# Split branch outputs taken straight from the banks of their transposes, with unit splits and a memset in other places of three stages

## The chip, the cores and the metric

The kernel runs on 1 core of one Trainium2 chip. The metric is the device time in microseconds (us) of one execution. Engines are called TensorE (PE in the profile, PEld its weight load), VectorE (DVE), ScalarE (ACT), GpSimd (POOL) and SyncE (SP).

## What is computed

Two layers of a decoder trunk over 256 tokens of width 1024, in float32. The reference, cut to the part that the change touches:

```python
for layer in range(DEPTH):                      # 2
    h = rms_norm(x, norm_mix[layer])
    proj = h @ w_in[layer]                      # qkv and gates of three branches
    o_a = gated_deltanet(...)                   # branch A, (1, 256, 512)
    o_b = hgrn2(...)                            # branch B
    o_c = dilated_attention(...)                # branch C, three groups of four heads
    mix = (gates[:, :, 0] * (o_a @ w_br_a[layer])
           + gates[:, :, 1] * (o_b @ w_br_b[layer])
           + gates[:, :, 2] * (o_c @ w_br_c[layer]))
    x = x + mix @ w_out[layer]
    h = rms_norm(x, norm_ffn[layer])
    # layer 0: x += SwiGLU(h); layer 1: x += top 2 of 8 SwiGLU experts
```

o_a and o_b end in `rms_norm(o, norm_g)` times a gate; norm_g is a gain per channel.

## The kernel before, in words

Each large product is made of three float32r products: both operands are split into a high and a low part, and hi x hi, hi x lo and lo x hi are added up (`products`, lines 466 to 470). The weights stream in **units** of 1 MB. SyncE loads unit u into one of 6 raw slots; ScalarE copies it to one of 3 `hi` slots (`prep`, line 1062), for which unit u-3 must have been used by TensorE; VectorE subtracts and leaves the low part in the raw slot (`prep`, line 1506); TensorE waits for both (`unit_ready`) and gives the unit back (`unit_over`). Each engine has its own instruction stream, written out by hand; `prep(n)` says at which places of it the next n units are split. The order of work is this order in the three streams and the semaphores between them; there is no planner.

One mixer layer uses 56 units. They are counted here from 0 in each layer.

**Branch A** (`deltanet`): TensorE transposes its output, normed and gated, into banks 4 and 5 (`turn_output`, line 694). ScalarE copies the two banks, times the gain, to the float32 tile `oT` (line 1266).

**Branch B** (`hgrn`): VectorE makes 1-f (`b_k`, line 1807), a clamp (line 1809), a memset of the attention tile (line 1811), one unit split, a running sum (line 1816) and a first difference. Then come turns n = 0 to 7: VectorE makes the two operands `b_qe` and `b_ke` of score product n+1, the next difference, a masked copy of score product n, and a unit split (two in turn 0). TensorE does score product n and one unit of 24 products in each turn (two units in turn 0), units 18 to 27 in all. After the last turn come the value products (24 matmuls), and ScalarE takes `b_o` out of banks 4 and 5, for norm and gate (`output_norm`).

**Branch C, first part** (`dilated`, the loop over three groups): TensorE uses six units in a turn (q, k, v of a group; units 28 to 45). ScalarE waits for branch B's output ahead of the loop (line 1307). In one turn ScalarE and VectorE split two units, square and norm q, split two, norm k, split two.

**Between the loop and the scores**: the halves of the split output of branch A, `o_hi[0]` and `o_lo[0]`, lie in the memory of `actT_hi`, and those of branch B in that of `actT_lo`; these are the operands of all of the input's products. So `split_branch(L, 0)` (ScalarE line 1338 and 1392, VectorE line 1878 and 1964) waits until unit 45 has been used, and splits `oT` there. Branch B's output is transposed after the loop too, copied to `oT`, and split after it (lines 1373 and 1930).

**Branch C, second part**: a loop written out, eight turns n (line 799), one for each of four heads in two blocks of tokens. TensorE: scores n+1, transposes of p, half a unit of branch A's or B's projection (`branch_part`, units 46 to 49), values n. VectorE: scaled scores n+1, and in even turns the gated product, then a unit split, and at the end of the turn `c_o` (line 1947), the output of head n. The transposes of the first block of `c_o` (`turn_oc`, line 811) come in turn 5. Units 50 to 55 follow in `project`.

In the last stage experts' chosen tokens are split into `e_hi` and `e_lo`, and their results into `y_hi` and `y_lo`.

Of the kernel before, what the change touches and what calls it, by code (L numbers as in the profile page):

```python
# [22 lines left out]
P = 128  # L23
# [128 lines left out]
def build(ctx, nc, dram):  # L152
# [44 lines left out]
    oT = sb("oT", [P, 3, H, T])  # L197
# [19 lines left out]
    b_o = sb("b_o", [P, TT, W], at=t0 + 8192)  # L217
# [15 lines left out]
    o_hi = [sb(f"o_hi{n}", [P, H, T], F32R, at=o0 + 8192 * n) for n in range(2)]  # L233
    o_lo = [sb(f"o_lo{n}", [P, H, T], F32R, at=o0 + 8192 * n + 4096) for n in range(2)]
    oc_hi = sb("oc_hi", [P, H, T], F32R, at=t0)
    oc_lo = sb("oc_lo", [P, H, T], F32R, at=t0 + 4096)
# [132 lines left out]
    oT_made = signal("oT_made", 2)  # L369
# [90 lines left out]
    def _(pe):  # L460
# [233 lines left out]
        def turn_output(L, br, src):  # L694

            pe.wait_ge(o_made.sem, o_made.at(L, br))
            for h in range(H):
                for t in range(TT):
                    a = src[:, t, h, :] if len(src.shape) == 4 else src[:, t, hs(h)]
                    ins = pe.transpose(PS[:, (4, 2)[br] + h // 2, ((h % 2) * TT + t) * P:((h % 2) * TT + t + 1) * P],  # L700
                                       a, ident)
# [3 lines left out]
        def hgrn(L):  # L705
# [3 lines left out]
            for n in range(LEVELS + 2):  # L709
# [27 lines left out]
        def dilated(L):  # L737
# [80 lines left out]
        def branch_c(L, k, t, js):  # L818
# [237 lines left out]
    def _(act):  # L1056
# [209 lines left out]
        def turn_output(L, br):  # L1266
            act.wait_ge(o_T.sem, o_T.at(L, 2 * br + 1))
            col = (R_GA, R_GB)[br] + L
            act.activation(oT[:, br, :, :].rearrange("p a b -> p (a b)"), bank(*((4, 5), (2, 3))[br]), COPY,
                           scale=small[:, col:col + 1]).then_inc(oT_made.sem, 1)  # L1270

        def hgrn(L):
# [22 lines left out]
            for n in range(LEVELS + 2):  # L1295
                prep(1 if n else 2)
# [9 lines left out]
        def dilated(L):  # L1306
            act.wait_ge(o_made.sem, o_made.at(L, 1))
            with prog.loop(act, GROUPS, 2) as g:
# [16 lines left out]
                prep(2)  # L1325
# [46 lines left out]
            act.wait_ge(oT_made.sem, oT_made.at(L, 1))  # L1372
            split_branch(L, 1)
            for n in range(TT * H):
# [3 lines left out]
                if n % 2 == 0:  # L1378
# [969 lines left out]
```

## Time and profile before

| | before |
|---|---|
| median of 3 runs (lowest to highest) | 2156.52 us (2156.25 to 2160.19) |
| the profiled execution, its own time | 2160.02 us |
| its span, first to last instruction | 2158.2 us |
| mean granted TensorE clock | 0.981 of full speed |
| TensorE, VectorE, ScalarE busy | 96%, 75%, 57% of the span |

The profiled execution is one of its own, beside the three runs. In rows of instructions the first number is the start in us from the start of the span, the second the duration; a pair of brackets at the end gives the time that the engine stood idle before the row and what ended it. Layer 0 of the mixers lies at about 20 to 460 us, layer 1 at 660 to 1108 us, experts behind it.

### The profile page before, as it was taken

Reading aid. Unit: us, or ns where it says so; the run is one execution under the profiler, and the core shown is the slowest. Engines: PE = TensorE matmul, PEld = TensorE weight load, DVE = VectorE, ACT = ScalarE, POOL = GpSimd, SP = SyncE. Lnnn points to the kernel's source line nnn. Section 1 sums busy time; section 2 is a strip of 40 time slices with the busy share of each in tenths; the row PEclk is TensorE's granted clock in tenths of the full one; section 3 lists DMA queues with packets and bytes.
Section 4 is the critical chain, followed back from the end, with each engine's and each line's share of the span. In section 5 each row is a group of like instructions: output and inputs, shape, how many; then the busy total and the mean of one; then the engine's idle time right before and its main releaser. Section 6 shows DMA issues by size and latency. Waiting matters only on the chain.

```text
span 2158.2 us, 29174 instructions
## 1 busy us (share of the span) xinstructions
PE 2065.2 (96%) x10899; PEld 1752.1 (81%) x10899; DVE 1612.2 (75%) x1256; ACT 1240.0 (57%) x1017; POOL 6.7 (0%) x12
## 2 busy tenths in 40 slices
PE   7999999989998999999979999999999999999997
PEld 6997887779997997887767888888888888888885
DVE  5878855745445878855766888898888889888886
ACT  4544455344433544455346767777676777767674
POOL 0000000000000000000000000000000000000000
PEclk9999999989999999999989999999999999999998
DMA  8423454245564523455237999999999999999995
GB/s 274 157 79 98 137 189 161 85 142 194 177 193 128 175 79 98 137 188 163 80 126 273 369 330 366 344 351 370 325 369 326 369 345 350 366 329 369 330 367 187
DMA packets 239201, 512.25 MB, mean 237 GB/s; under 512 B 11391, under 2 KB 34039, under 8 KB 239132
## 3 DMA queue, kind: packets, MB, share of 16 engines
q1 hardware_dynamic: 238124, 507.60, 67.6%
q0 software_dynamic: 1008, 3.69, 0.5%
q8 instruction: 48, 0.79, 0.2%
q14 instruction: 21, 0.17, 0.0%
HBM read 510.19 MB, written 1.07 MB: 237 GB/s over the span
## 4 chain that ended last, share of the span: by engine, by line
PE 85%; DVE 8%; issue 3%; ACT 2%; DMA 0%; DVEq 0%; SPq 0%; ACTq 0%
PE PS L468 25%; PE PS L470 25%; PE PS L469 25%; PE PS L539 6%; DVE lo L1511 3%; PE PS L940 1%; PE PS L977 1%; ACT hi L1070 1%; PE PS L488 1%; PE PS L953 0%; DVE a_act L1612 0%; DVE x L2031 0%; PE PS L750 0%; DMA rows<-in_knorm_c 0%; DVE t_n L1534 0%
## 5 line engine op out<-in xcount | busy, mean ns | idle before, releaser
L1511 DVE TENSOR_TENSOR lo<-raw,hi 128x2048 fp32r<-128x2048 f32 x481 | 1096.0, 2290 | 332.6 <-ACT hi L1070 329.5
L1070 ACT ACTIVATE hi<-raw 128x2048 fp32r<-128x2048 f32 x481 | 920.7, 1916 | 419.4 <-PE PS L470 413.7
L468 PE MATMUL PS<-hi,e_hi 128*128 128x512 f32 x896 | 358.7, 400 | 1.4 <-DVE e_lo L1534 1.4
L469 PE MATMUL PS<-lo,e_hi 128*128 128x512 f32 x896 | 354.3, 395 | 0.0
L470 PE MATMUL PS<-hi,e_lo 128*128 128x512 f32 x896 | 354.2, 395 | 0.0
L468 PE MATMUL PS<-hi,actT_hi 128*128 128x512 f32 x640 | 253.9, 397 | 2.9 <-ACT gate L1280 1.4
L470 PE MATMUL PS<-hi,actT_lo 128*128 128x512 f32 x640 | 249.6, 390 | 0.0
L469 PE MATMUL PS<-lo,actT_hi 128*128 128x512 f32 x640 | 249.1, 389 | 0.0
L468 PE MATMUL PS<-hi,fT_hi 128*128 128x512 f32 x536 | 210.1, 392 | 3.0 <-DVE fT_lo L1534 1.8
L469 PE MATMUL PS<-lo,fT_hi 128*128 128x512 f32 x536 | 209.2, 390 | 0.0
L470 PE MATMUL PS<-hi,fT_lo 128*128 128x512 f32 x536 | 208.9, 390 | 0.0
L468 PEld LDWEIGHTS PS<-hi,e_hi 128*128 128x128 f32 x896 | 169.1, 189 | 40.2 <-DVE e_lo L1534 1.6
L470 PEld LDWEIGHTS PS<-hi,e_lo 128*128 128x128 f32 x896 | 169.0, 189 | 40.2
L469 PEld LDWEIGHTS PS<-lo,e_hi 128*128 128x128 f32 x896 | 169.3, 189 | 37.7
L468 PE MATMUL PS<-actT_hi,hi 128*128 128x256 f32 x672 | 192.1, 286 | 2.5 <-DVE actT_lo L1585 1.4
L469 PE MATMUL PS<-actT_lo,hi 128*128 128x256 f32 x672 | 190.9, 284 | 0.0
L470 PE MATMUL PS<-actT_hi,lo 128*128 128x256 f32 x672 | 190.9, 284 | 0.0
L468 PEld LDWEIGHTS PS<-hi,actT_hi 128*128 128x128 f32 x640 | 120.4, 188 | 27.6 <-issue 4.3
L470 PEld LDWEIGHTS PS<-hi,actT_lo 128*128 128x128 f32 x640 | 120.1, 188 | 25.6
L469 PEld LDWEIGHTS PS<-lo,actT_hi 128*128 128x128 f32 x640 | 120.5, 188 | 23.9 <-issue 0.2
L468 PEld LDWEIGHTS PS<-actT_hi,hi 128*128 128x128 f32 x672 | 129.8, 193 | 4.0 <-DVE actT_lo L1585 1.8
L469 PEld LDWEIGHTS PS<-actT_lo,hi 128*128 128x128 f32 x672 | 129.8, 193 | 0.6 <-issue 0.2
(313 smaller groups left out, 2241.5 us busy)
## 6 DMA issues: line engine op xcount, KB each, us to landing
raw<-in_moe_w SPq DMA_DIRECT2D x336, 1024.0 KB, 5.1
raw<-in_w_in SPq DMA_DIRECT2D x92, 1024.0 KB, 5.1
raw<-in_ffn_w SPq DMA_DIRECT2D x33, 1024.0 KB, 5.3
raw<-in_w_br SPq DMA_DIRECT2D x12, 1024.0 KB, 5.1
raw<-in_w_out SPq DMA_DIRECT2D x8, 1024.0 KB, 5.2
hankel<-hankel_dram POOLq DMA_DIRECT2D x1, 1536.0 KB, 13.5
x<-in_x SPq DMA_DIRECT2D x2, 512.0 KB, 4.0
gain<-in_norm_mix POOLq DMA_DIRECT2D x2, 512.0 KB, 5.9
```

The costliest lines, as they stand in the source:

```text
L468: pe.matmul(out, a_hi, b_hi, start=first, stop=False, skip_group_check=True)
L469: pe.matmul(out, a_hi, b_lo, start=False, stop=False, skip_group_check=True)
L470: return pe.matmul(out, a_lo, b_hi, start=False, stop=last, skip_group_check=True)
L488: ins = pe.transpose(PS[:, 4 + j, (2 * kk + t) * P:(2 * kk + t + 1) * P], tile(t, k), ident)
L539: return pe.matmul(out, a, b, start=first, stop=last)
L940: ins = pe.matmul(PS[:, 6 + k // 4, (k % 4) * P:(k % 4 + 1) * P], src[:, t, k * P:(k + 1) * P], pick_r[:, t, :], start=t == 0 and part == ...
L977: ins = pe.transpose(PS[:, 2, j * P:(j + 1) * P], f_g[0][:, j * P:(j + 1) * P], ident)
L1070: act.activation(hi[prog.u % SPLIT][:, :], raw[slot][:, :], COPY).then_inc(hi_made.sem, 1)
L1511: dve.tensor_tensor(lo[prog.u % RAW][:, :], raw[prog.u % RAW][:, :], hi[s][:, :].bitcast(F32), ALU.subtract).then_inc(lo_made.sem, 1)
```

## The change

Branch A's output is transposed into banks 6 and 7 rather than 4 and 5. ScalarE copies these banks, times the gain, to `o_hi[0]` (float32r), and VectorE makes `o_lo[0]` from the same banks in `split_output(L, 0)`, both at the start of `hgrn`. The tiles take the place of `oT`. TensorE waits for the low part ahead of score product 1 (which writes banks 6 and 7), where before it waited for `oT` ahead of score product 0. Branch B's output is split in the same way from banks 2 and 3 after the loop, into the memory of `actT_hi`. Branch C's output later uses the tiles of branch A.

The memset of `b_attn` moves from the start of `hgrn` into turn 0, and one of the two unit splits of turn 0 goes; the loop over the groups splits three units ahead of the first norm and one after the second; in the eight turns a unit is split in turns 0, 1, 2, 4 and 6, and on VectorE it stands after `c_o`. The experts' split tiles move to the memory of `actT_hi` and `actT_lo`.

```diff
-    oT = sb("oT", [P, 3, H, T])
+    oa_hi = sb("oa_hi", [P, H, T], F32R)
+    oa_lo = sb("oa_lo", [P, H, T], F32R)
+    b_o = sb("b_o", [P, TT, W])
...
-    o_hi = [sb(f"o_hi{n}", [P, H, T], F32R, at=o0 + 8192 * n) for n in range(2)]
-    o_lo = [sb(f"o_lo{n}", [P, H, T], F32R, at=o0 + 8192 * n + 4096) for n in range(2)]
-    oc_hi = sb("oc_hi", [P, H, T], F32R, at=t0)
-    oc_lo = sb("oc_lo", [P, H, T], F32R, at=t0 + 4096)
+    o_hi = [oa_hi, sb("ob_hi", [P, H, T], F32R, at=o0)]
+    o_lo = [oa_lo, sb("ob_lo", [P, H, T], F32R, at=o0 + 4096)]
...
-    e_hi = sb("e_hi", [P, KT, P], F32R)
+    e_hi = sb("e_hi", [P, KT, P], F32R, at=o0)
...
 TensorE, turn_output
-                    ins = pe.transpose(PS[:, (4, 2)[br] + h // 2, ...
+                    ins = pe.transpose(PS[:, (6, 2)[br] + h // 2, ...
 TensorE, hgrn
-                    if n == 0:
-                        pe.wait_ge(oT_made.sem, oT_made.at(L, 0))
+                    if n == 1:
+                        pe.wait_ge(o_lo_made.sem, o_lo_made.at(L, 0))
 TensorE, values
                 if n == 0:
-                    pe.wait_ge(oT_made.sem, oT_made.at(L, 1))
+                    pe.wait_ge(o_lo_made.sem, o_lo_made.at(L, 1))
 ScalarE, turn_output
-            act.activation(oT[:, br, :, :].rearrange("p a b -> p (a b)"), bank(*((4, 5), (2, 3))[br]), COPY,
-                           scale=small[:, col:col + 1]).then_inc(oT_made.sem, 1)
+            act.activation(flat(o_hi[br]), bank(*((6, 7), (2, 3))[br]), COPY,
+                           scale=small[:, col:col + 1]).then_inc(o_hi_made.sem, 1)
 ScalarE, hgrn
             for n in range(LEVELS + 2):
-                prep(1 if n else 2)
+                prep(1)
 ScalarE, dilated, the loop over groups
-                prep(2)
+                prep(3)
                 square(0)
...
                 turned_c(1)
-                prep(1)
-
-            used(L, U_C + 18)
-            split_branch(L, 0)
             turn_output(L, 1)
...
             exps(0)
-            act.wait_ge(oT_made.sem, oT_made.at(L, 1))
-            split_branch(L, 1)
             for n in range(TT * H):
...
-                if n % 2 == 0:
+                if n % 2 == 0 or n == 1:
                     prep(1)
 VectorE, hgrn
-            dve.memset(flat(b_attn), 0.0).then_inc(dve_step.sem, 1)
-            dve.wait_ge(dve_step.sem, prog.step())
+            split_output(L, 0)
             prep(1)
...
+                if n == 0:
+                    dve.memset(flat(b_attn), 0.0).then_inc(dve_step.sem, 1)
+                    dve.wait_ge(dve_step.sem, prog.step())
                 masked(n)
-                prep(1 if n else 2)
+                prep(1)
 VectorE, dilated
-                prep(2)
+                prep(3)
                 normed(0)
                 prep(2)
                 normed(1)
-                prep(2)
-
-            split_branch(L, 0)
+                prep(1)
...
             scaled(0)
-            split_branch(L, 1)
+            split_output(L, 1)
             for n in range(TT * H):
...
                 if n % 2 == 0:
                     gated(L, n // 2, 3)
-                    prep(1)
...
                 dve.wait_ge(c_oc.sem, c_oc.at(L, n))
+                if n % 2 == 0 or n == 1:
+                    prep(1)
...
+        def split_output(L, br):
+
+            col = (R_GA, R_GB)[br] + L
+            dve.wait_ge(o_hi_made.sem, o_hi_made.at(L, br))
+            dve.scalar_tensor_tensor(flat(o_lo[br]), bank(*((6, 7), (2, 3))[br]), small[:, col:col + 1],
+                                     flat(o_hi[br]).bitcast(F32), ALU.mult, ALU.subtract).then_inc(o_lo_made.sem, 1)
```

## Rows read from the trace of the kernel before

**Rows 1.** The page's first part: busy us, share and instructions of each engine.

```profile
PE 2065.2 (96%) x10899; PEld 1752.1 (81%) x10899; DVE 1612.2 (75%) x1256; ACT 1240.0 (57%) x1017; POOL 6.7 (0%) x12
```

**Rows 2.** The waits of TensorE: total us, times, longest us.

```profile
PE PS L468 <- DVE o_lo L1534: 8.6, 2, 4.3
...
PE PS L815 <- DVE c_o L1947: 3.9, 2, 1.9
```

**Rows 3.** Timeline of TensorE, score products 2 and 8 of branch B, both layers.

```profile
207.83 3.58 PE L539 MATMUL PS<-b_qe,b_ke 128*128 128x128 f32 x16 [2.04 <-DVE b_ke L1534]
...
253.36 1.16 PE L539 MATMUL PS<-b_qe,b_ke 128*128 128x128 f32 x8
...
856.73 2.05 PE L539 MATMUL PS<-b_qe,b_ke 128*128 128x128 f32 x16 [2.04 <-DVE b_ke L1534]
...
901.03 1.16 PE L539 MATMUL PS<-b_qe,b_ke 128*128 128x128 f32 x8
```

**Rows 4.** Windows: length, busy us of each engine, granted clock, DMA share, GB/s.

```profile
208.00:212.00 4.00, 4.00 (x19) 3.92 (x20) 3.93 (x3) 1.26 (x2) 0.00 (x0) 0.57 0.61 233
373.50:378.00 4.50, 4.42 (x10) 3.47 (x11) 2.58 (x6) 1.66 (x3) 0.00 (x0) 0.50 0.00 0
1021.20:1026.00 4.80, 4.75 (x11) 3.78 (x12) 2.56 (x5) 1.66 (x3) 0.00 (x0) 0.50 0.00 0
```

**Rows 5.** Timeline of VectorE, start of branch B and turn 0, layer 0.

```profile
183.95 0.69 DVE L1809 TENSOR_SCALAR b_f<-b_f 128x1024 f32<-128x1024 f32 x1
185.03 1.34 DVE L1811 MEMSET b_attn<- 128x1536 f32 x1 [0.39 <-DVE b_f L1809]
...
188.62 2.86 DVE L1816 TENSOR_TENSOR_SCAN b_gc<-tiny,b_f 128x256 f32<-128x256 f32 x4
...
200.89 4.49 DVE L1511 TENSOR_TENSOR lo<-raw,hi 128x2048 fp32r<-128x2048 f32 x2
```

**Rows 6.** Timeline of ScalarE, start of branch B, layer 0.

```profile
183.15 1.12 ACT L1269 ACTIVATE oT<-PS,small 128x1024 f32<-128x1024 f32 x1 [3.70 <-PE PS L700]
184.16 1.91 ACT L1070 ACTIVATE hi<-raw 128x2048 fp32r<-128x2048 f32 x1
...
187.38 1.06 ACT L1276 ACTIVATE b_f<-b_f 128x1024 f32<-128x1024 f32 x1
```

**Rows 7.** Timelines of TensorE, ScalarE and VectorE, end of branch B, start of the group loop, layer 0.

```profile
259.85 2.84 PE L539 MATMUL PS<-b_i,b_attn 128*128 128x128 f32 x24
263.38 0.47 PE L468 MATMUL PS<-hi,actT_hi 128*128 128x512 f32 x1 [0.69 <-ACT gate L1280]
...
274.36 0.39 PE L468 MATMUL PS<-hi,actT_hi 128*128 128x512 f32 x1
...
260.10 1.91 ACT L1070 ACTIVATE hi<-raw 128x2048 fp32r<-128x2048 f32 x1 [4.57 <-PE PS L470]
...
262.82 1.02 ACT L1303 ACTIVATE b_o<-PS 128x1024 f32<-128x1024 f32 x1
...
270.84 1.92 ACT L1070 ACTIVATE hi<-raw 128x2048 fp32r<-128x2048 f32 x1 [2.79 <-DVE b_o L1534]
...
272.79 2.29 DVE L1511 TENSOR_TENSOR lo<-raw,hi 128x2048 fp32r<-128x2048 f32 x1 [2.23 <-ACT hi L1070]
```

**Rows 8.** Timelines of VectorE and TensorE, after the group loop, layer 0.

```profile
372.31 1.22 DVE L1534 TENSOR_TENSOR o_lo<-oT,o_hi 128x1024 fp32r<-128x1024 f32 x1
...
373.58 0.80 PE L468 MATMUL PS<-hi,o_hi 128*128 128x512 f32 x1 [4.33 <-DVE o_lo L1534]
```

**Rows 9.** Timelines of VectorE and ScalarE, turns 0 and 1 of the eight, layer 0.

```profile
373.44 0.42 DVE L1890 SCALAR_TENSOR_TENSOR c_s<-PS,bias 128x256 f32<-128x256 f32 x1
373.89 0.29 DVE L1895 SCALAR_TENSOR_TENSOR c_s<-PS,bias 128x128 f32<-128x128 f32 x1
...
374.99 0.61 ACT L1354 ACTIVATE c_p<-c_s,stat 128x384 f32<-128x384 f32 x1 [2.98 <-DVE stat L1900]
...
382.84 1.22 DVE L1972 SCALAR_TENSOR_TENSOR gate<-gate,PS 128x1024 f32<-128x1024 f32 x1 [1.56 <-PE PS L470]
```

More of the change, by code:

```diff
@@ L216, in build @@
     b_e = sb("b_e", [P, H, T], at=c0 + 6144)
-    b_o = sb("b_o", [P, TT, W], at=t0 + 8192)
     b_o2 = sb("b_o2", [P, TT, W], at=c0 + 14336)
@@ L261, in build @@
     pickT = sb("pickT", [P, TT, P], F32R)
-    e_hi = sb("e_hi", [P, KT, P], F32R)
-    e_lo = sb("e_lo", [P, KT, P], F32R)
-    y_hi = sb("y_hi", [P, D], F32R)
-    y_lo = sb("y_lo", [P, D], F32R)
+    e_hi = sb("e_hi", [P, KT, P], F32R, at=o0)
+    e_lo = sb("e_lo", [P, KT, P], F32R, at=o0 + 4096)
+    y_hi = sb("y_hi", [P, D], F32R, at=o0 + 8192)
+    y_lo = sb("y_lo", [P, D], F32R, at=o0 + 12288)
     PS = ctx.enter_context(nc.psum_tensor("PS", [P, 8, 512], F32))
@@ L368, in build @@
     o_T = signal("o_T", 6)
-    oT_made = signal("oT_made", 2)
     bf_read = signal("bf_read")
@@ L699, in turn_output @@
                     a = src[:, t, h, :] if len(src.shape) == 4 else src[:, t, hs(h)]
-                    ins = pe.transpose(PS[:, (4, 2)[br] + h // 2, ((h % 2) * TT + t) * P:((h % 2) * TT + t + 1) * P],
+                    ins = pe.transpose(PS[:, (6, 2)[br] + h // 2, ((h % 2) * TT + t) * P:((h % 2) * TT + t + 1) * P],
                                        a, ident)
@@ L825, in branch_c @@
             for j in js:
-                ins = products(PS[:, (6, 0)[k] + t, :], oc_hi[:, j, t * P:(t + 1) * P],
-                               oc_lo[:, j, t * P:(t + 1) * P], unit_view(w_hi, 4)[:, j, :],
+                ins = products(PS[:, (6, 0)[k] + t, :], o_hi[0][:, j, t * P:(t + 1) * P],
+                               o_lo[0][:, j, t * P:(t + 1) * P], unit_view(w_hi, 4)[:, j, :],
                                unit_view(w_lo, 4)[:, j, :], first=j == 0, last=j == H - 1)
@@ L1360, in split_oc @@
                 act.wait_ge(o_T.sem, o_T.at(L, 4 + t))
-                act.activation(oc_hi[:, :, t * P:(t + 1) * P], PS[:, 2, :].rearrange("p (h j) -> p h j", h=H),
+                act.activation(o_hi[0][:, :, t * P:(t + 1) * P], PS[:, 2, :].rearrange("p (h j) -> p h j", h=H),
                                COPY).then_inc(o_hi_made.sem, 1)
@@ L1388, in dilated @@
             prep(1)
-        def split_branch(L, br):
-            act.activation(flat(o_hi[br % 2]), oT[:, br, :, :].rearrange("p a b -> p (a b)"),
-                           COPY).then_inc(o_hi_made.sem, 1)
         def dense():
@@ L1905, in split_oc @@
                 v = slice(t * P, (t + 1) * P)
-                tt(oc_lo[:, :, v], bank4(2), oc_hi[:, :, v].bitcast(F32), ALU.subtract).then_inc(o_lo_made.sem, 1)
+                tt(o_lo[0][:, :, v], bank4(2), o_hi[0][:, :, v].bitcast(F32), ALU.subtract).then_inc(o_lo_made.sem, 1)
             def gated_c(k, t):
@@ L1960, in dilated @@
             prep(2)
-        def split_branch(L, br):
+        def split_output(L, br):
+            col = (R_GA, R_GB)[br] + L
             dve.wait_ge(o_hi_made.sem, o_hi_made.at(L, br))
-            tt(flat(o_lo[br % 2]), oT[:, br, :, :].rearrange("p a b -> p (a b)"),
-               flat(o_hi[br % 2]).bitcast(F32), ALU.subtract).then_inc(o_lo_made.sem, 1)
+            dve.scalar_tensor_tensor(flat(o_lo[br]), bank(*((6, 7), (2, 3))[br]), small[:, col:col + 1],
+                                     flat(o_hi[br]).bitcast(F32), ALU.mult, ALU.subtract).then_inc(o_lo_made.sem, 1)
         def gated(L, k, pair):
```

## The prediction

> **What bounds the kernel.** I read the page's first part: TensorE is busy for 96% of the span, VectorE for 75% [rows 1]. So the time is TensorE's work plus its stops and slow stretches, and only what shortens those counts. The list of TensorE's waits and its timeline give three that this change touches: 8.6 us in two stops for `o_lo`, 3.9 us in two stops for `c_o` [rows 2], and two stops of 2.04 for `b_ke` [rows 3]; one of each in each layer. They lie ahead of score product 2 of branch B [rows 3], ahead of the first product of branch A's projection [rows 8], and at the transposes of `c_o` in turn 5. Windows of the clock show what a stop costs beyond itself [rows 4]: behind the 4.3 us stops TensorE ran at 1.2 GHz (0.50) for at least 4.5 and 4.8 us; behind the 2.0 us stop it was at 0.57 over 4 us in layer 0, while in layer 1 the same product took 2.05 us rather than 3.58 [rows 3], so was at full clock. Stops of 2 us can thus cost clock, or not.
>
> **Change, part 1: start of branch B.** VectorE's chain from 183.95 to 207.8 has no idle time to speak of. The memset took 1.34 us after 0.39 of start [rows 5]. The new split in its place starts at 184.66, since `o_hi` is ready at 184.3 [rows 6], and I take 1.22 us, the price of another three-operand instruction on two banks [rows 9]. A split between SBUF tiles took 1.22 too [rows 8]. Bounds: 0.69 (a one-operand instruction of that size, rows 5) to 2.3 (twice the elements, rows 5). It ends at 185.9; the unit split then waits for ScalarE's `hi` until 186.1 and ends at 188.4; the running sum waits for ScalarE's logarithm, which ends at 188.44 [rows 6]. So it starts at 188.5 rather than 188.62: 0.15 us are gained, not 0.4, since ScalarE is late next. Turn 0 then loses one of two unit splits (4.49 for two, so 2.2, rows 5) and gains the memset (1.35). Together `b_ke` of turn 1 comes 0.15 + 2.2 - 1.35 = 1.0 us sooner. TensorE's stop shrinks from 2.04 to 1.0.
>
> What of it lasts? In layer 1 product 2 to product 8 took 44.3 us, 7.38 per turn [rows 3]. A unit of 24 products takes 5.49 (half of 274.36 - 263.38, rows 7) and 16 score matmuls 1.8, together 7.3: VectorE sets the pace by a hair, and whatever it gains early arrives at the end. Layer 1 gains 1.0. In layer 0 the same stretch took 45.5 because of the slow clock. A stop of 1.0 should not slow it: 1.0 + 1.2 = 2.2. TensorE's new wait for `o_lo` ahead of product 1 costs nothing: it is made 12 us sooner; behind it only product 1 is queued. Banks 6 and 7 are free, as product 1 is their next writer.
>
> **Part 2: end of branch B.** One unit fewer is now ahead. ScalarE's split at 260.10, which waited 4.57 us for TensorE and kept the last gate and so TensorE's first product of the loop waiting (0.69) [rows 7], is one unit earlier in number and waits for nothing: that 0.69 goes. But unit 30, split there before, is now the first split behind ScalarE's wait for branch B's output. Its `hi` starts where unit 31's did, at 270.84, its low part ends where 272.79 + 2.29 = 275.08 stands, both 0.1 sooner since `b_o` no longer waits for the gate [rows 7]. TensorE comes from its value products (262.69) through two units (10.98) to 273.67, and **stops for 1.3 us**, a new stop. It goes on at 275.0 rather than 274.36: +0.65 in each layer. In the loop the order of splits against norms is as before (three, two, one instead of two, two, two, over the turn's border), and I put it at nothing: TensorE's six units cover it, and the units stay two ahead. If that cover is gone it costs a stop like the 1.3 in each of three turns.
>
> **Part 3: after the loop.** The splits of `oT` (VectorE's is 1.22, rows 8), the wait for unit 45 and the unit split ahead of them leave the path: `o_lo[0]` is made a hundred us earlier. TensorE goes from score product 0 straight into the projection: -4.33 and -4.3. The slow clock behind it goes as well: half of 4.5 and of 4.8 us [rows 4], -2.25 and -2.4. Branch B's split (copy 1.1, low part 1.22) lies under the first half unit; values 0 waits for it, 6 us later.
>
> **Part 4: the eight turns.** With `c_o` ahead of the unit split, the transposes in turn 5 should not stop for 1.94. But a fifth split stands in turn 1. Worked there: from the maximum of scores 2 come ScalarE's exponential (0.61 and some 0.1 for its sum), its `hi` (1.92, rows 7), VectorE's low part (2.29), scaled scores 3 (0.42 + 0.29) [rows 9] and hand-overs of 0.1 to 0.2 in all, 5.8 us, where TensorE has 4.6 of work (half a unit 2.75, the rest small products): a stop of 1.2. Going through all turns like this I find stops of 0.5, 1.2, 0.4, 1.3 and 0.9, 4.3 us, in turns 1 to 4, none in turn 5. The same walk in the old order gives 4.3 as well (the trace has 3.8). I take **0**, with 2 us a layer either way as bounds.
>
> Moved tiles of the experts carry no instruction and no wait: 0. No DMA is added or moved; SyncE's loads follow the use of raw slots, six ahead, and POOL waits for the same fourth low part.
>
> **A rule against the change.** The rows show 1.22 us for 1024 elements from SBUF and from banks alike [rows 8, 9]. The Trainium skill, "VectorE: DVE Perf Modes", section on the TRN2 errata, gives an instruction a larger fixed cost if it reads PSUM (120 cycles against 58). By it each of four splits would cost some 0.06 us more, an estimate from that page, and the sum would be 0.1 to 0.25 us less of a gain. The trace does not agree for this size.
>
> **Sum.** Layer 0: -2.2 + 0.65 - 4.33 - 2.25 = -8.1. Layer 1: -1.0 + 0.65 - 4.3 - 2.4 = -7.1. Together -15.2, from the profiled execution's 2160.0 (span 2158.2 and 1.8 around it): 2144.8. That execution is 3.5 above the median of 2156.5; the slow clock of layer 0 at 208 us, 1.2 of my sum, need not be in the others, as layer 1 shows. From the median I take off 14.0: **2142.5 us**.
>
> **Rivals.**
> 1. *The new stops cost clock.* The 1.3 us stop at unit 30, or those of turns 2 to 4 close together, bring 1.2 GHz in both layers, at about 2.3 us each [rows 4]: 2147. For it: 2.04 did so once. Against: once only, and that was longer. Chance 0.15.
> 2. *The next wait takes the place.* TensorE still stops for 4.3 us after the loop, for scores or for VectorE. Then 4.3 + 2.3 stay in both layers: 2142.5 + 13.3 = 2155.8, no change to be seen. Against: the copy for scores 0 is ready, and scaled scores 0 come sooner, as nothing is queued ahead of them. Chance 0.04.
> 3. *More.* Unit 30 is not late, or the eight turns gain their 1.94: 2142.5 - 2.6 or - 3.9, so 2139. Chance 0.14.
> 4. *Slower: the missing unit.* In branch B's turns a unit is split one turn before its use; `hi` and low part take 4.2 of 7.4 us, so 3.2 are in hand. If raw data or ScalarE come later than that, each of 8 turns and 3 loop turns waits in both layers. It outweighs the gain from 14 / 22 = 0.65 us per turn; at 1.3 us, as at unit 30, it gives 2142.5 + 28 = 2171. Against: ScalarE stood idle for 4.57 us with all tiles full [rows 7]. Chance 0.02.
>
> **How the numbers follow.** Forecast 0.65. About 0.2% (4.3 us) can be told from no change: 2152.2 is the border. Faster: forecast, rivals 1 and 3, together 0.94, less 0.01 for several small ones at once: 0.93. Same: rival 2 and that 0.01: 0.05. Slower: 0.02. The range: forecast with 2 us either way per layer in the turns, half of rival 1's cost beyond it and rival 3's gain: 2138 to 2148.5.
>
> **What would show it.** Right: no wait of TensorE for `o_lo` of some 4 us; the projection's first products at clock 1.00; the stop at product 2 about 1.0 and at full clock; a new stop for `lo` of 1.3 us some 11 us into the group loop; no wait for `c_o` in turn 5 but several of about 1 us for `c_s` and `c_p`. Wrong: a stop of 3 us or more after the loop, waits for `lo` in more than one turn of the loop, or the memset's place on VectorE making product 2 later than before.

## The result, and the profile after

| | before | after |
|---|---|---|
| median of 4 runs (lowest to highest) | 2156.44 us (2156.25 to 2160.19) | 2128.22 us (2127.38 to 2129.13) |
| ratio of the runs, with its 95% interval | | 0.9859 (0.9848 to 0.9871) |
| the profiled execution, its own time | 2160.02 us | 2127.89 us |
| its span | 2158.2 us | 2126.1 us |
| mean granted TensorE clock | 0.981 | 0.988 |

The time fell by 28.2 us, twice the forecast 14.0. In lines of the kernel after, `prep` is L1068 on ScalarE and L1499 on VectorE, the products are L466 to L468, the small matmuls L537. First the page's busy times, which answer to [rows 1]: TensorE lost 24 us of busy time with the same number of matmuls.

```profile
PE 2041.0 (96%) x10899; PEld 1742.6 (82%) x10899; DVE 1610.7 (76%) x1256; ACT 1234.3 (58%) x1013; POOL 6.7 (0%) x12
```

TensorE's waits after, total, times and longest. No `o_lo` and no `c_o` is left of [rows 2]; the waits for `lo` hold the new stops at unit 30.

```profile
PE PS L466 <- DVE lo L1499: 7.5, 11, 1.5
...
PE PS L537 <- DVE c_s L1884: 3.7, 4, 1.0
...
PE PS L537 <- DVE b_ke L1522: 2.9, 2, 1.4
...
PE PS L779 <- ACT c_p L1349: 2.4, 4, 0.7
```

The timeline of TensorE after, at score product 2 of both layers (against [rows 3]) and at unit 30, the third of the group loop (against [rows 7]).

```profile
207.05 2.05 PE L537 MATMUL PS<-b_qe,b_ke 128*128 128x128 f32 x16 [1.43 <-DVE b_ke L1522]
...
273.06 0.47 PE L466 MATMUL PS<-hi,actT_hi 128*128 128x512 f32 x1 [1.54 <-DVE lo L1499]
...
845.76 2.05 PE L537 MATMUL PS<-b_qe,b_ke 128*128 128x128 f32 x16 [1.43 <-DVE b_ke L1522]
...
911.80 0.47 PE L466 MATMUL PS<-hi,actT_hi 128*128 128x512 f32 x1 [1.54 <-DVE lo L1499]
```

Both stops are those forecast (1.0 and 1.3 us), a little longer. Windows of the kernel after, in the same three places as [rows 4] (length, busy times, granted clock, DMA share, GB/s): the clock stays at 1.00 where it was 0.57, 0.50 and 0.50.

```profile
207.00:211.00 4.00, 3.95 (x25) 3.59 (x26) 3.90 (x3) 2.68 (x3) 0.00 (x0) 1.00 0.80 256
369.00:373.50 4.50, 4.50 (x26) 3.85 (x25) 3.29 (x8) 1.59 (x4) 0.00 (x0) 1.00 0.08 30
1009.00:1014.00 5.00, 5.00 (x32) 4.41 (x31) 2.61 (x7) 2.77 (x6) 0.00 (x0) 1.00 0.00 0
```

**Where the time went.** The row that ends branch A (transposes of `t_n`) and the first transposes of each norm (`fn`, `hn`) cut the span into stages. TensorE's timeline before, then after:

```profile
182.02 0.66 PE L700 MATMUL PS<-consts,t_n 128*128 128x128 f32 x4 [0.81 <-DVE t_n L1534]
...
465.14 3.67 PE L488 MATMUL PS<-consts,fn 128*128 128x128 f32 x16 [6.76 <-DVE fn L1552]
668.35 1.97 PE L488 MATMUL PS<-consts,hn 128*128 128x128 f32 x8 [9.30 <-DVE hn L1552]
1113.31 3.03 PE L488 MATMUL PS<-consts,fn 128*128 128x128 f32 x13 [6.76 <-DVE fn L1552]
```

```profile
181.85 0.88 PE L698 MATMUL PS<-consts,t_n 128*128 128x128 f32 x6 [0.82 <-DVE t_n L1522]
...
456.58 3.68 PE L486 MATMUL PS<-consts,fn 128*128 128x128 f32 x16 [6.75 <-DVE fn L1540]
657.98 3.67 PE L486 MATMUL PS<-consts,hn 128*128 128x128 f32 x16 [9.30 <-DVE hn L1540]
1095.33 3.47 PE L486 MATMUL PS<-consts,fn 128*128 128x128 f32 x16 [6.75 <-DVE fn L1540]
```

| stage (from row to row, the last to the span's end) | before | after | difference |
|---|---|---|---|
| mixer 0 behind branch A | 283.12 | 274.73 | -8.4 |
| dense stage | 203.21 | 201.40 | -1.8 |
| mixer 1 | 444.96 | 437.35 | -7.6 |
| last norm and experts | 1044.9 | 1030.8 | -14.1 |

The stages and 0.2 us ahead of them make up the 32.1 us between the two profiled spans; the medians differ by 28.2, as the profiled execution before was 3.6 above its median. The mixers gained 16.0 us, where the sum had 15.2. The other 16 us lie in stages in which, by the forecast, nothing moves; most of it with the experts. TensorE's groups of products there, before and then after (count, busy us, mean ns, idle time before them):

```profile
L468 PE MATMUL PS<-hi,e_hi 128*128 128x512 f32 x896 | 358.7, 400 | 1.4 <-DVE e_lo L1534 1.4
L469 PE MATMUL PS<-lo,e_hi 128*128 128x512 f32 x896 | 354.3, 395 | 0.0
L470 PE MATMUL PS<-hi,e_lo 128*128 128x512 f32 x896 | 354.2, 395 | 0.0
```

```profile
L466 PE MATMUL PS<-hi,e_hi 128*128 128x512 f32 x896 | 354.8, 396 | 1.4 <-DVE e_lo L1522 1.4
L468 PE MATMUL PS<-hi,e_lo 128*128 128x512 f32 x896 | 349.8, 390 | 0.0
L467 PE MATMUL PS<-lo,e_hi 128*128 128x512 f32 x896 | 349.4, 390 | 0.0
```

And a window of 950 us in that stage, before, then after: the clock is 1.00 and TensorE busy for over 99.7% in both, but it did 4390 matmuls instead of 4333.

```profile
1150.00:2100.00 950.00, 948.32 (x4333) 776.01 (x4332) 823.67 (x482) 680.69 (x455) 0.00 (x0) 1.00 0.97 352
```

```profile
1150.00:2100.00 950.00, 947.61 (x4390) 785.45 (x4389) 832.33 (x485) 689.59 (x460) 0.00 (x0) 1.00 0.97 355
```

The 2688 products take 13.2 us less in sum (1067.2 against 1054.0), 4.9 ns each. In such a product (128x512) TensorE holds 128 columns of the split tokens and streams 512 of the split weight, so the suspect is the one part of the change that carries no instruction: the place of `e_hi` and `e_lo`.

### The profile page after: what moved, and what is told of

It reads as the page before. It is cut to its first block, busy times and chain, and to the rows that moved or that the text cites. A ratio compares the mean times of both kernels' runs of the same rounds, so it can differ in the third digit from the quotient of the medians.

```text
span 2126.1 us, 29178 instructions
## 1 busy us (share of the span) xinstructions
PE 2041.0 (96%) x10899; PEld 1742.6 (82%) x10899; DVE 1610.7 (76%) x1256; ACT 1234.3 (58%) x1013; POOL 6.7 (0%) x12
## 4 chain that ended last, share of the span: by engine, by line
PE 85%; DVE 8%; issue 3%; ACT 2%; DMA 0%; DVEq 0%; SPq 0%; ACTq 0%
PE PS L466 25%; PE PS L468 24%; PE PS L467 24%; PE PS L537 7%; DVE lo L1499 3%; PE PS L938 1%; PE PS L975 1%; ACT hi L1068 1%; PE PS L486 1%; PE PS L748 0%; DVE x L2022 0%; DVE a_act L1600 0%; PE PS L951 0%; DMA rows<-in_knorm_c 0%; PE PS L779 0%
## 5 line engine op out<-in xcount | busy, mean ns | idle before, releaser
L1499 DVE TENSOR_TENSOR lo<-raw,hi 128x2048 fp32r<-128x2048 f32 x481 | 1094.6, 2289 | 301.1 <-ACT hi L1068 298.5
L1068 ACT ACTIVATE hi<-raw 128x2048 fp32r<-128x2048 f32 x481 | 919.4, 1915 | 339.6 <-PE PS L468 334.0
L466 PE MATMUL PS<-hi,e_hi 128*128 128x512 f32 x896 | 354.8, 396 | 1.4 <-DVE e_lo L1522 1.4
L468 PE MATMUL PS<-hi,e_lo 128*128 128x512 f32 x896 | 349.8, 390 | 0.0
L467 PE MATMUL PS<-lo,e_hi 128*128 128x512 f32 x896 | 349.4, 390 | 0.0
L466 PE MATMUL PS<-hi,actT_hi 128*128 128x512 f32 x640 | 253.9, 397 | 4.6 <-DVE lo L1499 4.1
L468 PE MATMUL PS<-hi,actT_lo 128*128 128x512 f32 x640 | 249.6, 390 | 0.0
L466 PE MATMUL PS<-hi,fT_hi 128*128 128x512 f32 x536 | 210.3, 392 | 4.2 <-DVE lo L1499 2.4
L468 PE MATMUL PS<-hi,fT_lo 128*128 128x512 f32 x536 | 209.3, 390 | 0.0
L466 PEld LDWEIGHTS PS<-hi,e_hi 128*128 128x128 f32 x896 | 168.6, 188 | 37.1 <-issue 2.1
L468 PEld LDWEIGHTS PS<-hi,e_lo 128*128 128x128 f32 x896 | 168.4, 188 | 35.9
L466 PE MATMUL PS<-actT_hi,hi 128*128 128x256 f32 x672 | 191.3, 285 | 2.5 <-DVE actT_lo L1573 1.4
L468 PE MATMUL PS<-actT_hi,lo 128*128 128x256 f32 x672 | 190.2, 283 | 0.0
L466 PEld LDWEIGHTS PS<-hi,actT_hi 128*128 128x128 f32 x640 | 120.3, 188 | 29.7 <-ACT hi L1068 3.9
L468 PEld LDWEIGHTS PS<-hi,actT_lo 128*128 128x128 f32 x640 | 120.1, 188 | 25.6
L466 PEld LDWEIGHTS PS<-actT_hi,hi 128*128 128x128 f32 x672 | 128.9, 192 | 4.1 <-DVE actT_lo L1573 1.8
```

What stands on the lines that cost most here:

```text
L466: pe.matmul(out, a_hi, b_hi, start=first, stop=False, skip_group_check=True)
L467: pe.matmul(out, a_hi, b_lo, start=False, stop=False, skip_group_check=True)
L468: return pe.matmul(out, a_lo, b_hi, start=False, stop=last, skip_group_check=True)
L1068: act.activation(hi[prog.u % SPLIT][:, :], raw[slot][:, :], COPY).then_inc(hi_made.sem, 1)
L1499: dve.tensor_tensor(lo[prog.u % RAW][:, :], raw[prog.u % RAW][:, :], hi[s][:, :].bitcast(F32), ALU.subtract).then_inc(lo_made.sem, 1)
```

## Experiments: the experts' tiles

**The tiles back, and the tiles alone.** In the changed kernel (first run) the four tiles went back:

```diff
-    e_hi = sb("e_hi", [P, KT, P], F32R, at=o0)
-    e_lo = sb("e_lo", [P, KT, P], F32R, at=o0 + 4096)
-    y_hi = sb("y_hi", [P, D], F32R, at=o0 + 8192)
-    y_lo = sb("y_lo", [P, D], F32R, at=o0 + 12288)
+    e_hi = sb("e_hi", [P, KT, P], F32R)
+    e_lo = sb("e_lo", [P, KT, P], F32R)
+    y_hi = sb("y_hi", [P, D], F32R)
+    y_lo = sb("y_lo", [P, D], F32R)
```

> The changed kernel with the experts' split tokens and their split products (four tiles, 16 KB) back behind the kernel's last tile, nothing else undone. Between the two traces each expert's period fell from 125.6 us to 124.1 us (eight of them, 12 us) though no instruction of the experts changed, only the place of these tiles. Theory A (the place of the tiles sets how fast TensorE takes them): the period returns to 125.6 us, the products whose held operand is a split token to 0.400 / 0.395 us, and the time is 2128.2 + 12 = 2140 us (0.5% over the changed kernel). Theory B (something else that differs between the kernels, such as where the instructions lie or what memory the rest uses): 2128 us, period 124.1 us, as after.

The second run made the reverse edit in the kernel before, in these four lines alone.

> The kernel before with these four tiles laid over the split layer input, nothing else changed. Theory A (place of the tiles): expert period 124.1 us, time 2156.4 - 12 = 2144 us, ratio to before 0.994. Theory B (something else): 2156 us, period 125.6 us.

Measured: 2140.14 us (ratio to before 0.9912, 0.9895 to 0.9928), means 401 / 396 / 396 ns; and 2148.58 us (0.9947, 0.993 to 0.9963; before had 2159.95 in that session), means 397 / 391 / 391. Both by theory A: +11.9 and -11.4 us. The place of these tiles is worth 12 us in either kernel.

**Which tiles, and what of their place.** Third run: only `e_hi` and `e_lo` back.

```diff
-    e_hi = sb("e_hi", [P, KT, P], F32R, at=o0)
-    e_lo = sb("e_lo", [P, KT, P], F32R, at=o0 + 4096)
+    e_hi = sb("e_hi", [P, KT, P], F32R)
+    e_lo = sb("e_lo", [P, KT, P], F32R)
```

> The changed kernel with only the split tokens (e_hi, e_lo) back at their old address; the split products (y_hi, y_lo) stay where the change put them. If it is the operand that TensorE holds (the token tiles): 2140 us, period 125.6 us. If it is the tiles that VectorE and ScalarE write at the end of an expert: 2128 us. If both share it: between.

Fourth: the same, behind a tile of 128 bytes per partition.

> As the last run, but with 128 bytes per partition ahead of the split tokens, so that they lie high in the memory as before but at the same offset within 512 bytes as in the changed kernel. Theory A1 (the offset within 512 bytes decides): 2128 us, period 124.1 us. Theory A2 (the region of the memory decides): 2140 us, period 125.6 us.

```diff
+    pad = sb("pad", [P, 32])
     e_hi = sb("e_hi", [P, KT, P], F32R)
     e_lo = sb("e_lo", [P, KT, P], F32R)
```

Measured: 2140.52 us and 2128.33 us. So it is the tokens, not `y_hi` and `y_lo`, and not the region of the memory: 128 bytes further on in the same region give back all 12 us.

**An absolute offset, or one against the streamed tile?** The split weights lie at offset 128 within 512 bytes, where the tokens are cheap. Two kernels tell which: `e_hi` at 64 and `e_lo` at 256; and the tokens at 0 with all of weights' ring, their split tiles and `actT` at 0 too.

```diff
+    e0 = cursor - (cursor & 511)
-    e_hi = sb("e_hi", [P, KT, P], F32R, at=o0)
-    e_lo = sb("e_lo", [P, KT, P], F32R, at=o0 + 4096)
+    e_hi = sb("e_hi", [P, KT, P], F32R, at=e0 + 576)
+    e_lo = sb("e_lo", [P, KT, P], F32R, at=e0 + 4608 + 256)
```

> The changed kernel, with e_hi (the rounded half of the split tokens) at an offset of 64 bytes within 512 and e_lo at 256, both high in the memory. Known so far, mean of one product: e_hi at offset 0 0.400 and 0.395 us and e_lo 0.395; at offset 128 0.396, 0.390 and 0.390. If only offset 0 is dear: 0.396 / 0.390 / 0.390, 2128 us. If only offset 128 (or the same offset as the split weights, which lie at 128) is cheap: 0.400 / 0.395 / 0.395, 2140 us. One of each gives one operand each way.

In the other, `e_hi` and `e_lo` go back as in the third run, and:

```diff
+    lb = sb("lb", [P, 8, H])
+    tiny = sb("tiny", [P, 8])
+    stat = sb("stat", [P, 16])
     w0 = cursor
     raw = [sb(f"raw{s}", [P, UE]) for s in range(RAW)]
...
-    lb = sb("lb", [P, 8, H])
-    tiny = sb("tiny", [P, 8])
-    stat = sb("stat", [P, 16])
```

> The changed kernel with the split tokens back at their old place (offset 0 within 512 bytes) and three small tiles (384 bytes) laid ahead of all others, so that the weights' ring, their split tiles and the mixers' split input lie at offset 0 too instead of 128; the dense stage's held tiles fT_hi, fT_lo stay at 128. Theory held-tile (a product costs 5 ns more whenever the tile that TensorE holds starts at offset 0): split tokens 0.400 / 0.395, actT products 0.397 to 0.402 and 0.390 to 0.395, the 128x256 products 0.283 to 0.288 (there the split weight is held), dense products stay 0.392 / 0.390; (1920 + 2016 products) x 4.7 ns = 18 us more than 2140: 2158 us. Theory distance (dear is a held tile at another offset than the streamed one): split tokens and actT 0.396 / 0.390, dense products dear, (3 x 536) x 4.7 ns = 7.6 us on 2128: 2136 us. Theory streamed tile (the offset of the split weights counts too): anything else, the products' means say which.

Measured: 2142.8 us, 401 / 396 / 396 ns (both dear), and 2137.21 us, where the theory of the distance had 2136. TensorE's groups of the second:

```profile
L466 PE MATMUL PS<-hi,e_hi 128*128 128x512 f32 x896 | 355.0, 396 | 1.4 <-DVE e_lo L1522 1.4
L468 PE MATMUL PS<-hi,e_lo 128*128 128x512 f32 x896 | 350.3, 391 | 0.0
L467 PE MATMUL PS<-lo,e_hi 128*128 128x512 f32 x896 | 350.0, 391 | 0.0
...
L466 PE MATMUL PS<-hi,fT_hi 128*128 128x512 f32 x536 | 212.9, 397 | 4.3 <-DVE lo L1499 2.6 <-DVE fT_lo L1522 1.8
L467 PE MATMUL PS<-lo,fT_hi 128*128 128x512 f32 x536 | 211.6, 395 | 0.0
```

The tokens at offset 0 are cheap now, and the dense stage's held tiles, which were not moved, became dear (397 / 395 against 392 / 391). The theory of the held tile's own offset falls; the distance to the streamed tile stands.

**Which distances?** Three runs, each with the edit of the run at 64 and 256, and other numbers: 384 and 512 + 160; 384 and 384; 512 + 160 and 512 + 160.

> Held and streamed tile's offsets within 512 bytes, so far: equal (128/128, 0/0) 0.390 us, held 64, 128 or 384 bytes on from the streamed one 0.395. Here e_hi lies 256 on from the split weights (384 against 128) and e_lo 32 on (160 against 128). If only equal offsets are cheap: 0.400 / 0.395 / 0.395, 2140 us. If the distance counts modulo 256: e_hi 0.396 / 0.390 and e_lo 0.395: 2128 + 4 = 2132 us. If small distances are cheap too: e_lo 0.390.

> e_hi and e_lo both 256 bytes on from the split weights (384 against 128 within 512). If only equal offsets are cheap: 0.400 / 0.395 / 0.395, 2140 us. If the distance counts modulo 256 (oa_hi lies at 384 too, and its few products took 0.389): 0.396 / 0.390 / 0.390, 2128 us.

> e_hi and e_lo both 32 bytes on from the split weights (160 against 128). If only equal offsets are cheap: 2140 us. If distances under 64 bytes are cheap as well: 2128 us.

| held `e_hi`, `e_lo` / streamed weights, within 512 | distance | mean ns of the three products | time, us |
|---|---|---|---|
| 128, 128 / 128 (after, and high in memory) | 0 | 396, 390, 390 | 2128.2, 2128.3 |
| 0, 0 / 0 (all shifted) | 0 | 396, 391, 391 | 2137.2, with the dense stage dear |
| 384, 384 / 128 | 256 | 396, 390, 390 | 2129.3 |
| 160, 160 / 128 | 32 | 401, 396, 396 | 2141.4 |
| 64, 256 / 128 | -64, 128 | 401, 396, 396 | 2142.8 |
| 0, 0 / 128 (as before) | -128 | 401, 396, 395 | 2140.5 |
| 384, 160 / 128 | 256, 32 | 400, 400, 390 | 2139.4 |

All but the kernels of the first row and the one at -128 ran once each; the four runs of each of the kernels above spread over at most 2.7 us, and the difference in question is 12. The mixed pair (last line) went by none of its three theories: `e_hi`, at distance 256, is dear in both of its products and `e_lo`, at 32, is cheap, the reverse of what the rows above say; its total is a dear one. When both tiles lie at the same distance, it is clear: 0 and 256 are cheap, and every other distance tried costs 4.4 to 5.5 ns a product (7.0 us over the 1608 products of the dense stage with all shifted, 14.7 over the 2688 of the experts at 32 against 256). That 256 counts as 0 rests on one kernel, and on the changed kernel's branch products: those of `oa_hi`, at distance 256, take the same 389 and 393 ns as those of `ob_hi`, at 0. TensorE's groups at distance 256, then at 32:

```profile
L467 PE MATMUL PS<-hi,e_hi 128*128 128x512 f32 x896 | 354.9, 396 | 1.4 <-DVE e_lo L1523 1.4
L469 PE MATMUL PS<-hi,e_lo 128*128 128x512 f32 x896 | 349.8, 390 | 0.0
```

```profile
L467 PE MATMUL PS<-hi,e_hi 128*128 128x512 f32 x896 | 359.0, 401 | 1.4 <-DVE e_lo L1523 1.4
L469 PE MATMUL PS<-hi,e_lo 128*128 128x512 f32 x896 | 355.0, 396 | 0.0
```

## Experiments: units, splits and memset in the mixers

The stages in the table are measured as in the one above, each kernel in its own profiled execution.

| kernel | mixer 0 | mixer 1 | time, us (ratio to before, interval) |
|---|---|---|---|
| before | 283.12 | 444.96 | 2156.44 |
| after | 274.73 | 437.35 | 2128.22 (0.9848 to 0.9871) |
| memset back | 274.37 | 436.70 | 2126.86 (0.9831 to 0.9863) |
| splits from a copy | 276.23 | 438.84 | 2134.45 (0.9865 to 0.9898) |
| all units back | 280.91 | 442.36 | 2142.25 (0.9911 to 0.9944) |
| units back but in the loop | 295.63 | 457.91 | 2171.15 (1.0033 to 1.0069) |
| wait and memset placed anew | 271.24 | 433.48 | 2121.86 (0.9807 to 0.984) |
| and VectorE's units | 267.73 | 429.98 | 2115.05 (0.9783 to 0.982) |

**The memset back** to the start of branch B:

```diff
             dve.wait_ge(b_clamp.sem, b_clamp.at(L))
+            dve.memset(flat(b_attn), 0.0).then_inc(dve_step.sem, 1)
+            dve.wait_ge(dve_step.sem, prog.step())
             split_output(L, 0)
...
-                if n == 0:
-                    dve.memset(flat(b_attn), 0.0).then_inc(dve_step.sem, 1)
-                    dve.wait_ge(dve_step.sem, prog.step())
```

> The changed kernel with the memset of b_attn back at the start of branch B, ahead of the split of branch A's output, nothing else undone. Theory A (it stood in the chain to b_ke): the products that open the loop come 1.34 + 0.39 us later where VectorE has no slack, so TensorE waits some 1.4 us at score product 1 or 2 more than in the changed kernel, and its clock may fall again: 1.7 to 4 us a layer, at the changed kernel's 2128 + 3 to 8 = about 2132 us. Theory B (VectorE is waiting for ScalarE there anyway): 2128 us, and the stop at score product 2 of 1.43 us gets shorter, as the memset no longer lies ahead of the unit's split.

TensorE's timeline, score products 1 and 2 of layer 0:

```profile
198.98 2.05 PE L537 MATMUL PS<-b_qe,b_ke 128*128 128x128 f32 x16 [0.89 <-DVE b_ke L1522]
...
206.36 2.05 PE L537 MATMUL PS<-b_qe,b_ke 128*128 128x128 f32 x16
```

The stop moved from product 2 to product 1 and went from 1.43 to 0.89. Neither theory had it whole. Moving the memset into turn 0 gained nothing: the mixers are 0.4 and 0.6 us longer with it there and the median 1.4 us, at the edge of what the runs can tell.

**The splits made from a copy, as before; units, memset and tiles as changed:**

```diff
             act.wait_ge(o_T.sem, o_T.at(L, 2 * br + 1))
-            act.activation(flat(o_hi[br]), bank(*((6, 7), (2, 3))[br]), COPY,
-                           scale=small[:, col:col + 1]).then_inc(o_hi_made.sem, 1)
+            act.activation(flat(oT[br]), bank(*((6, 7), (2, 3))[br]), COPY,
+                           scale=small[:, col:col + 1]).then_inc(oT_made.sem, 1)
+        def split_branch(L, br):
+            act.activation(flat(o_hi[br]), flat(oT[br]), COPY).then_inc(o_hi_made.sem, 1)
...
                 turned_c(1)
+            used(L, U_C + 18)
+            split_branch(L, 0)
             turn_output(L, 1)
...
 VectorE
-            split_output(L, 0)
             prep(1)
...
                 prep(1)
+            split_output(L, 0)
...
+            tt(flat(o_lo[br]), flat(oT[br]), flat(o_hi[br]).bitcast(F32), ALU.subtract)
```

> The changed kernel with only the splits of the two branch outputs made as before: ScalarE copies the transposes' banks to memory, rounds from the copy behind the group loop (branch A) and behind the first exps (branch B), VectorE subtracts from the copy behind the group loop and behind the first scores. The places of the units, of the memset and of the experts' tiles stay as changed. Theory A (the prediction's third part: these splits set the 4.3 us stop ahead of the first branch product and the slow clock behind it): a stop of 3 to 5 us on o_lo in each layer and 2.3 us of clock, less the new stop at score product 2 (1.43 us), which has VectorE's split of branch A no longer ahead of it: 2128 + 2 x (4.3 + 2.3 - 1.4) = 2138 us. Theory B (the stop was due to the units that stood in the same queues, and these are moved): 2125 to 2129 us.

TensorE's timeline at the first branch product:

```profile
370.17 0.50 PE L468 MATMUL PS<-hi,oa_hi 128*128 128x512 f32 x1 [1.27 <-DVE oa_lo L1531]
```

The stop is 1.27 us, not 4.33, and the score product 2 stops for 1.44 as in the changed kernel. The run lies between the theories. Its span is 7.9 us over that after: 3.0 in the mixers, and 2.0 in the dense stage, 2.1 behind the last mixer and 0.9 ahead of branch B, three stretches in which no edit was made.

**All units back** where they stood; splits, memset and tiles as changed:

```diff
 ScalarE and VectorE, hgrn
-                prep(1)
+                prep(1 if n else 2)
 ScalarE, dilated
-                prep(3)
+                prep(2)
                 square(0)
...
                 turned_c(1)
+                prep(1)
...
-                if n % 2 == 0 or n == 1:
+                if n % 2 == 0:
                     prep(1)
 VectorE, dilated
-                prep(3)
+                prep(2)
                 normed(0)
                 prep(2)
                 normed(1)
-                prep(1)
+                prep(2)
...
                     gated(L, n // 2, 3)
+                    prep(1)
...
-                if n % 2 == 0 or n == 1:
-                    prep(1)
```

> The changed kernel with all unit splits where they stood before (two in branch B's first turn; 2-2-2 on VectorE and 2-2-1-1 on ScalarE in the group loop; four in the eight turns, on VectorE ahead of c_o); the direct splits, the memset and the tiles stay as changed. Theory A (the splits straight from the banks carry the gain in the mixers): the stops return to the gate stop of 0.69, c_o of 1.95 and one of 2 to 3.7 us at score product 2, the c_n stops of run g1 do not come: 2128 + 2 x (2 + 1.1) = 2134 us. Theory B (the moved units carry it): the time comes to 2156.4 - 12 (tiles) = 2144 us.

Timelines of VectorE and TensorE behind the group loop, then the transposes in turn 5:

```profile
372.64 2.29 DVE L1500 TENSOR_TENSOR lo<-raw,hi 128x2048 fp32r<-128x2048 f32 x1 [5.17 <-ACT hi L1068]
374.85 0.42 DVE L1880 SCALAR_TENSOR_TENSOR c_s<-PS,bias 128x256 f32<-128x256 f32 x1
...
375.65 0.94 PE L537 MATMUL PS<-c_kT,c_qT 128*128 128x128 f32 x6 [1.10 <-DVE c_s L1885]
...
407.80 0.66 PE L813 MATMUL PS<-consts,c_o 128*128 128x128 f32 x4 [1.94 <-DVE c_o L1937]
```

2142.25 us, near theory B. The stops are nevertheless those that theory A lists (0.69, 1.94 and 3.65 us), with 1.10 for `c_s` beside them, and the clock fell behind the longest: its 16 matmuls took 3.79 us. Its sum is 8 us too low all the same. VectorE's last unit of the loop (372.64) now delays the first scaled scores instead of `o_lo`, and in branch B product 2 stops for 3.65 us, more than the 2.04 of [rows 3], as the memset stands there too. The mixers take 4.8 us less than before with the splits and the memset, 13.0 less with the units and the memset, 16.0 with all. The first figure is held down by the memset, whose new place, with two units in the same turn, makes the stop at product 2 longer by 1.6 us in each layer; the splits without it were not run.

**Units back in the first turn and the eight turns, but not in the group loop** (the last diff without the lines around `square(0)`, `turned_c(1)`, `normed(0)` and `normed(1)`):

> The changed kernel with the unit splits back in branch B's first turn (two) and in the eight turns (four, on VectorE ahead of c_o); the group loop keeps its new 3-2-1. Theory A (the prediction's parts 1 and 4: one in the first turn costs more at score product 2, and in the eight turns the placement is worth nothing, 3.8 against 3.0 us of stops): 2 x (2.2 + 0.8) = 6 us more and clock of some 2 us in each layer where the stop passes 2 us: 2134 to 2138 us. Theory B (VectorE has the room in either place): 2128 us.

2171.15 us, slower than the kernel before, by a mechanism that neither theory had. TensorE's waits, and timelines of ScalarE, VectorE and TensorE ahead of the first norm in the loop:

```profile
PE PS L748 <- DVE c_n L1522: 23.4, 12, 1.9
```

```profile
281.46 1.92 ACT L1068 ACTIVATE hi<-raw 128x2048 fp32r<-128x2048 f32 x1 [3.52 <-PE PS L468]
...
283.28 1.00 ACT L1312 ACTIVATE c_sq<-PS 128x1024 f32<-128x1024 f32 x1
...
283.41 2.29 DVE L1499 TENSOR_TENSOR lo<-raw,hi 128x2048 fp32r<-128x2048 f32 x1 [3.15 <-ACT hi L1068]
...
288.81 1.50 PE L748 MATMUL PS<-consts,c_n 128*128 128x128 f32 x7 [1.95 <-DVE c_n L1522]
```

With one unit more split ahead of the loop, the third unit ahead of the norm has no free `hi` slot: ScalarE waits 3.52 us for TensorE, with the squares queued behind it, and `c_n` is 1.95 us late, 12 times. One unit fewer ahead of the loop and three ahead of the first norm belong together.

**Going on from the changed kernel.** First ScalarE's wait, which guards `c_sq` alone, behind three unit roundings, and the memset, of the two chunks that need it, ahead of a wait in which VectorE idles; then also VectorE's units behind turns 1, 3, 4, 6 and 7.

```diff
         def dilated(L):
-            act.wait_ge(o_made.sem, o_made.at(L, 1))
...
                 prep(3)
+                act.wait_ge(o_made.sem, o_made.at(L, 1))
                 square(0)
...
         def hgrn(L):
+            dve.memset(b_attn[:, 0:2].rearrange("p c h j -> p (c h j)"), 0.0).then_inc(dve_step.sem, 1)
+            dve.wait_ge(dve_step.sem, prog.step())
             dve.wait_ge(o_T.sem, o_T.at(L, 1))
...
-                if n == 0:
-                    dve.memset(flat(b_attn), 0.0).then_inc(dve_step.sem, 1)
-                    dve.wait_ge(dve_step.sem, prog.step())
```

> An attempt to go on: the changed kernel with ScalarE's wait for branch B's output moved behind three unit roundings (it guards c_sq alone), and the memset, of the two thirds that need it, ahead of VectorE's wait for the transposes of branch A, where VectorE idles 1.26 us. If the two new stops (1.54 us at unit 30, 1.43 us at score product 2) come from these two placements they go, in both layers: 2 x 2.97 = 5.9 us, 2122 us. If the next wait in the chain takes their place: 2125 to 2128 us.

2121.86 us: both stops are gone in both layers (score product 2 at 205.33, no idle time before it).

```diff
-                if n % 2 == 0 or n == 1:
+                if n in (1, 3, 4, 6, 7):
                     prep(1)
```

> The last attempt (2121.9 us) with VectorE's five unit subtractions in the eight turns behind turns 1, 3, 4, 6 and 7 instead of 0, 1, 2, 4 and 6; ScalarE's stay. An event model built from the two traces' durations gives 3.5 us less for each layer, but it has the stops of the changed kernel at 4.6 us where the trace has 3.0. Theory A (the 0.87 and 0.95 us stops on c_s come from a subtraction standing ahead of the scaling of the next turn's scores): they go, and the time is 2121.9 - 2 x (1.8 to 3.5) = 2115 to 2118 us. Theory B (a later unit then comes too late for TensorE): a new stop on lo, 2120 to 2126 us.

2115.05 us, theory A: no stop of TensorE above 0.3 us for `c_s` or `c_p` is left in the turns of layer 0, and the stop that takes their place is half a microsecond. From TensorE's waits:

```profile
PE PS L466 <- DVE oa_lo L1522: 0.9, 2, 0.5
```

This version beats both kernels: 13 us less than the change, 2.0% less than before.

## Why the prediction was wrong

The direction and the mixers were right, the total was not: 2128.2 lies outside 2138.0 to 2148.5.

**The step that failed** is the sentence "Moved tiles of the experts carry no instruction and no wait: 0". It priced an edit of addresses by its instructions. It was worth -12 us, shown from both sides (+11.9 undone, -11.4 alone). Without it, the changed kernel took 2140.1 us, 2.4 below the forecast and inside its range. That it comes so near is in part luck: the stop at product 2 shrank by 0.6 us instead of 1.0 and unit 30 cost 0.2 us more than forecast, while the eight turns gave some 0.8 us a layer that the sum had at nothing.

**Part 1** (-2.2 and -1.0): the stop at product 2 is 1.43, forecast 1.0, at full clock as said. The memset's share was misjudged. At the old place the sum counts 0.39 us of start beside its 1.34, in turn 0 it counts 1.35 alone; but the 0.39 comes along, and is the 0.4 by which the stop is longer than forecast. The memset's new place brought nothing, and the gain came from the one unit less: with two units there the stop is 3.65. VectorE after, turn 0:

```profile
199.53 1.34 DVE L1844 MEMSET b_attn<- 128x1536 f32 x1 [0.39 <-DVE b_e L1522]
```

That `o_lo` costs 1.22 is nearly so: the rows have 1.28 for branch A and 1.27 for branch B, from banks. By an estimate from the page that the forecast names (the Trainium skill, "VectorE: DVE Perf Modes", section on the TRN2 errata) it would be 0.06 more than between SBUF tiles, and here the trace agrees in size, though the instruction differs in more than its source, and [rows 9] has 1.22 from a bank.

**Part 2** (+0.65 a layer): the gate's stop went, the stop at unit 30 came, 1.54 instead of 1.3. That order in the group loop costs nothing is right for this kernel only: the run with one unit more ahead shows the price, 23.4 us, if the cover is gone. The prediction looked for it in units that come too late; it came from a unit too many ahead, for which the `hi` slots were still in use.

**Part 3** (-4.33, -4.3 and the clock): the stop and the slow clock went, as forecast. The text names the splits and the unit split ahead of them in one list and doesn't say what each is worth. The runs take them away one at a time: with the units moved and the splits through a copy the stop is 1.27 us, with the old units and the direct splits 1.10 (for `c_s`), with both edits none. So either edit alone takes 3.1 to 3.2 of the 4.33 us, and neither can be called the cause by itself.

**Part 4** (0, within 2): stops of 0.53, 0.87, 0.95 and 0.68, together 3.0 where before had 3.8; none in turn 5. Forecast were five, together 4.3: one of 0.4 did not come, and the three behind the first were taken 0.2 to 0.35 us too long.

**The clock.** Beyond the mixers, the dense stage and the stretch at the last norm gave back 1.8 and 2.3 us. There TensorE waits for a norm in both kernels, but behind the dense stage's norm the clock was 0.57 before (470 to 475 us) and 1.00 after (461.5 to 466.5 us). [rows 4] names other places, and the prediction has no term for it. The runs spread: 201.2 to 203.4 us for the same dense stage. What decides it was not tried.

**Rivals.** 1 (clock lost by new stops): no, stops up to 1.54 us left it at 1.00. 2: no. 3 (more): its named reasons did not come, except 0.8 us a layer in the turns; what came is the place of the tiles. 4 (slower by missing units): not in this kernel.

## What to carry to other kernels

When a tile moves, note the address of what TensorE holds against what it streams at the time; equal offsets cost nothing to arrange, and here they were worth 0.6%. Units split ahead and slots to hold them are one plan: move a split in one stage and recount the slots in the next. Before a stop is put down to the instruction that it names, list what else stands in that queue, and take away one at a time: here either of two edits would have taken three quarters of the stop.

## What the runs showed of the hardware

Where all held tiles of a stage lie at distance 0 or 256 from the streamed ones (within 512 bytes), a product of 128x512 takes 4.4 to 5.5 ns less than at distances of 32, 64 or 128 bytes, from start to start about 0.228 us instead of 0.233, at the same clock (1.00). It holds for tokens against weights at two absolute offsets, and for the dense stage, whose products became dear when the weights moved away from them. TensorE's loads and products overlap (PEld is busy for 82% of the span and PE for 96%); that the two reads collide would fit; it was argued and not shown, and the mixed pair (400, 400, 390) is not explained by a cost that belongs to each product by itself. The 64 products of the experts' results (`y_hi`, `y_lo` streamed) can't be used for it: their means are 398 and 395 ns after and 423 and 424 ns in the run with the memset back, with every tile of theirs at the same address. What moves them was not pursued.

Stops near 2 us cost clock by turns. In the run with twelve stops of 1.95 us the granted clock fell behind the one ahead of each first norm and stayed at 1.00 behind the one ahead of each second. Windows of that kernel, behind the first two stops:

```profile
289.00:293.00 4.00, 4.00 (x16) 3.43 (x16) 2.29 (x1) 0.30 (x1) 0.00 (x0) 0.57 0.66 245
304.50:308.50 4.00, 4.00 (x22) 3.45 (x23) 2.29 (x1) 2.31 (x3) 0.00 (x0) 1.00 0.63 236
```

The Trainium skill, "TensorE: Matmul & The Clock Gate", section "Step-by-step: what each phase is for", says that TensorE has two independent read ports into SBUF and that "Loading the next tile's weights doesn't steal SBUF read bandwidth from the running matmul". That sentence names no reason for the place of a tile to matter; these runs measured 12 us for it, and none of them shows whether the two reads are what costs it.
